# Block with four mixers on one Trainium2 core: head norms by strips, and delta-rule operands in exchanged halves

## The reference

```python
def l2norm(x, eps=1e-6):
    return x * rsqrt(sum(x * x, axis=-1) + eps)

def gated_deltanet(qkv, a_logit, b_logit, z, ...):
    q, k, v = split(silu(causal_depthwise_conv(qkv, conv_w)))
    q = l2norm(heads(q)) * HEAD_DIM ** -0.5
    k = l2norm(heads(k))
    g = -exp(a_log) * softplus(a_logit + dt_bias)
    o = chunked_gated_delta_rule(q, k, v, g, sigmoid(b_logit))
    return rmsnorm(o, norm_w) * silu(heads(z))

def spatial_gating(u, v, z, ...):
    v = layernorm(heads(gelu(v)), ln_gain, ln_bias, 1e-5)
    mixed = einsum('gts,bnsgc->bntgc', tril(w_s), v) + b_s
    return gelu(u) * mixed * silu(z)

def rwkv7_time_mix(rw, z, mu, ...):
    rw = rw + mu * (shift_prev(rw) - rw)
    r, k, v, wd, ad = split(rw)
    decay = exp(-exp(-softplus(-(w0 + tanh(wd) @ w_up)) - 0.5))
    a = sigmoid(a0 + ad @ a_up)
    kk = l2norm(heads(k * k_k))
    k = k * (1 + (a - 1) * k_a)
    o = rwkv7_scan(r, decay, k, v, kk, a)
    o = layernorm(o, gn_gain, gn_bias, 64e-5) + sum(r * k * r_k, -1) * v
    return o * silu(z)
```

## Time and profile before

| what | value |
|---|---|
| median of 3 runs | 2642.43 us (2641.89 to 2644.74) |
| the profiled execution, its own time | 2643.93 us |
| span of its trace | 2642.6 us |
| mean granted clock of TensorE | 0.958 |
| TensorE (PE) busy | 2408.1 us, 91% |
| weight loads (PEld) busy | 1046.9 us, 40%, beside PE |
| VectorE (DVE) busy | 930.5 us, 35% |
| ScalarE (ACT) busy | 497.8 us, 19% |
| DMA | 556.51 MB, mean 211 GB/s |

### The profile page before, as it was taken

How to read it: one execution, slowest core, us unless ns; L and a number is a source line. 1 busy time by engine, 2 the same in 40 slices (tenths; PEclk the granted TensorE clock), 3 DMA queues, 4 the chain that set the end, 5 groups by cost and what they waited for, 6 DMA issues and landing times.

```text
span 2642.6 us, 27853 instructions
## 1 busy us (share of the span) xinstructions
PE 2408.1 (91%) x11714; PEld 1046.9 (40%) x11714; DVE 930.5 (35%) x1538; ACT 497.8 (19%) x823; POOL 0.2 (0%) x4
## 2 busy tenths in 40 slices
PE   6899989699999999986999999989998699998698
PEld 1344345233333333432333333334443246754443
DVE  4548652411111115644012111131017755417652
ACT  2246100211011011022101101120014322114500
POOL 0000000000000000000000000000000000000000
PEclk9899999899999999998999999989999899998799
DMA  7134411599999974415899999912222111023042
GB/s 280 72 143 151 159 64 56 211 421 421 421 422 421 421 316 191 173 66 208 350 421 421 421 421 422 406 38 79 72 76 74 48 61 50 24 64 121 1 159 80
DMA packets 96858, 556.51 MB, mean 211 GB/s; under 512 B 13561, under 2 KB 14073, under 8 KB 40219
## 3 DMA queue, kind: packets, MB, share of 16 engines
q1 hardware_dynamic: 90432, 538.77, 51.7%
q10 hardware_dynamic: 6300, 15.95, 1.6%
HBM read 544.19 MB, written 10.49 MB: 210 GB/s over the span
## 4 chain that ended last, share of the span: by engine, by line
PE 80%; DVE 13%; ACT 4%; issue 2%; DMA 0%; ACTq 0%; DVEq 0%; SPq 0%
PE bank L205 78%; PE bank L208 2%; DVE residual L1371 1%; DVE rms L1709 1%; DVE scores L2465 1%; DVE proj L431 1%; DVE topk L1267 0%; DVE squares L1337 0%; DVE max L1266 0%; ACT squares L1331 0%; ACT wring L1299 0%; ACT L1668 0%; ACT scores_t L2510 0%; DVE cf_y L1563 0%; DVE proj L1709 0%
## 5 line engine op out<-in xcount | busy, mean ns | idle before, releaser
L205 PE MATMUL bank<-normed,wring 128*128 128x512 f32 x1712 | 779.3, 607 | 11.1 <-DVE proj_small L2676 3.8
L205 PEld LDWEIGHTS bank<-normed,wring 128*128 128x128 f32 x1712 | 322.6, 193 | 408.1 <-issue 392.6
L205 PE MATMUL bank<-experts,wring 128*64 128x512 f32 x2048 | 445.8, 593 | 1.8 <-ACT wring L1313 1.8
L1337 DVE TENSOR_TENSOR squares<-squares,bank 128x512 f32<-128x512 f32 x32 | 22.0, 688 | 676.1 <-ACT squares L1331 676.1
L205 PEld LDWEIGHTS bank<-experts,wring 128*64 128x64 f32 x2048 | 145.5, 137 | 287.0 <-issue 284.8
L205 PE MATMUL bank<-experts,hs_t 128*64 128x512 f32 x1024 | 223.3, 594 | 1.5 <-ACT hs_t L1352 1.5
L205 PE MATMUL bank<-give_t,y 128*128 128x512 f32 x256 | 128.6, 621 | 10.2 <-DVE residual L1371 5.9
L205 PEld LDWEIGHTS bank<-experts,hs_t 128*64 128x64 f32 x1024 | 72.1, 137 | 141.3 <-issue 139.4
L1371 DVE SCALAR_TENSOR_TENSOR residual<-bank,mods,residual 128x512 f32<-128x512 f32 x128 | 96.1, 751 | 69.9 <-PE bank L205 64.2
L205 PE MATMUL bank<-h_tm,pick 128*128 128x512 f32 x256 | 117.6, 614 | 2.4 <-DVE pick L1279 2.4
L205 PE MATMUL bank<-proj,wring 128*128 128x512 f32 x224 | 99.4, 597 | 1.6 <-DVE proj L2563 1.6
(11 more groups left out here) (469 smaller groups left out, 2090.4 us busy)
## 6 DMA issues: line engine op xcount, KB each, us to landing
experts<-in_exp_w SPq DMA_DIRECT2D x384, 1024.0 KB, 15.1
wring<-in_w_in SPq DMA_DIRECT2D x82, 512.0 KB, 3.5
residual<-in_w_mod SPq DMA_DIRECT2D x24, 1024.0 KB, 6.6
cf_wmod<-in_w_mod SPq DMA_DIRECT2D x16, 1024.0 KB, 5.7
wring<-in_cf_w SPq DMA_DIRECT2D x24, 512.0 KB, 3.5
wmod<-in_w_mod SPq DMA_DIRECT2D x8, 1024.0 KB, 10.0
merge_gates<-squares ACTq DMA_DIRECT2D x32, 256.0 KB, 2.5
proj<-merge_gates SPq DMA_DIRECT2D x8, 1024.0 KB, 6.4
```

The lines of the kernel that those rows point to most:

```text
L205: return self.nc.tensor.matmul(out, lhsT, rhs, start=start, stop=stop, skip_group_check=True)
L1337: k.vec(v.tensor_tensor(m.hs[:, e, :], m.hs[:, e, :], k.bank[3 - 2 * e][:, :], ALU.mult), f"{m.name}.hs{i}.{e}")
```

## The change

**Head norms.** For the sums of squares, four products of 128x32 (stationary, from a new constant tile `heads`) by 128x128 a chunk put the chunk's sums in four strips of 32 partitions of one 128x128 tile: row 32g + 8i + 4h is token group g, chunk i, head h (`head_strips_tensor`). Up to four chunks add into the same tile. One mean, one root and one reciprocal of 128x128 follow (`head_roots`), then VectorE spreads the roots over 512 columns (L1743 of the changed kernel), and one product of 128x512 a chunk spreads them over the head's rows (`head_spread_tensor`). VectorE scales from PSUM with the gain in the same instruction (`head_scaled_vector`). The squares are made on ScalarE (`head_square_scalar`). The spatial mixer's bias is added on ScalarE. The sums for centring stay as they were, but the four Gelus are in another order (the two that are waited for come first), and one more DMA (`heads`, 128x644) is issued ahead of them. In gdn's preparation six more filler steps are drawn in its six convolution rounds; the spatial mixer draws one step fewer.

**Delta rule.** `m` and `u` of the levels are written to the other half of the partitions (`OTHERS`) by products whose input and output halves differ, and so are `x` of the chunks, the transposed `bv` of gdn, and the first level's transposed copies, for which there is a second set of 64x512 products. `products_tensor` takes several products and interleaves them: `m` of pair p+1 and `t` of pair p go call by call. The order is now m0, (m1, t0), u0, (m2, t1), u1, (m3, t2), u2, t3, u3.

**Memory.** `rw_up` and `rw_scratch` have no buffers of their own any more and lie in `mixer_out`.

The diff, cut:

```diff
+def head_constants():
+
+
+    p, j = np.arange(P)[:, None], np.arange(32)[None, :]
+    sums = [(j // 8 == i) * (j % 8 // 4 == p // 64) for i in range(4)]
+    rows = [p % 32 == 8 * i + 4 * (np.arange(P)[None, :] // 64) for i in range(4)]
+    return np.concatenate(sums + rows + [p // 32 == np.arange(4)[None, :]], 1).astype(np.float32)
...
-        self.up = d.sb("rw_up", [P, 256])
-        self.z3 = d.sb("rw_scratch", [P, T])
+        self.z3, self.up = self.ys[:, 4, :], self.ys[:, 5, 0:256]
...
+def head_strips_tensor(k, m, name, i, after, src, b, last):
+    t = k.nc.tensor
+    t.wait_ge(*k.at(after))
+    for g in range(4):
+        ins = k.mm(k.bank[b][32 * g:32 * g + 32, 0:P], m.heads[:, 32 * i:32 * i + 32], src[:, g * P:(g + 1) * P], i == 0, last)
+    if last:
+        ins.then_inc(*k.up("tensor", f"{name}.strips"))
...
+    k.vec(v.reciprocal(rt, rt))
+    k.vec(v.tensor_tensor(fm3(rs, 4), rt.unsqueeze(1).broadcast_to([P, 4, P]),
+                          m.heads[:, 640:644].unsqueeze(2).broadcast_to([P, 4, P]), ALU.mult), f"{name}.roots")
...
+def head_spread_tensor(k, m, name, i, rs, b):
+    k.nc.tensor.wait_ge(*k.at(f"{name}.roots"))
+    k.mm(k.bank[b][:, :], m.heads[:, (i + 1) * P:(i + 2) * P], rs).then_inc(*k.up("tensor", f"{name}.spread{i}"))
...
+def head_scaled_vector(k, name, i, x, gain, b):
+    v = k.nc.vector
+    v.wait_ge(*k.at(f"{name}.spread{i}"))
+    k.vec(v.scalar_tensor_tensor(out=x, in0=x, scalar=gain, in1=k.bank[b][:, :], op0=ALU.mult, op1=ALU.mult), f"{name}.scaled{i}")
...
-def gdn_prepare_tensor(k, m):
+def squares_of(m):
+    return m.kh[:, 0, :], m.kh[:, 1, :], m.bv[:, 0, :], m.bv[:, 1, :]
+
+
+def gdn_prepare_tensor(k, m, filler):
     t, bank, PJ, SL = k.nc.tensor, k.bank, m.pj, m.sl
     B, BB, E = (PJ[:, 8 + i, :] for i in range(3))
-    yield from steps_of(6)
-    for c in range(4):
-        yield from head_sums_tensor(k, f"gp.sum{c}", f"gp.sq{c}", B, 0)
-        yield
+    for c in range(6):
+        if 1 <= c <= 4:
+            head_strips_tensor(k, m, "gp", c - 1, f"gp.sq{c - 1}", squares_of(m)[c - 1], 0, c == 4)
+        next(filler, None)
+        yield
+    yield
+    yield
+    head_spread_tensor(k, m, "gp", 0, m.ys[:, 1, :], 1)
+    head_spread_tensor(k, m, "gp", 1, m.ys[:, 1, :], 2)
+    yield
+    t.wait_ge(*k.at("gp.scaled1"))
+    head_spread_tensor(k, m, "gp", 2, m.ys[:, 1, :], 1)
+    head_spread_tensor(k, m, "gp", 3, m.ys[:, 1, :], 2)
...
+        if c < 4:
+            head_square_scalar(k, f"gp.sq{c}", f"gp.silu{c}", squares_of(m)[c], PJ[:, c, :])
+        next(filler, None)
...
+    head_mean_vector(k, "gp", 0, 1.0, 1e-6, m.rt[:, 0, :])
+    yield
+    head_root_vector(k, m, "gp", m.rt[:, 0, :], m.ys[:, 1, :])
+    yield
+    for c in range(2):
+        head_scaled_vector(k, "gp", c, PJ[:, c, :], HD ** -0.5, 1 + c)
+    yield
+    for c in range(2, 4):
+        head_scaled_vector(k, "gp", c, PJ[:, c, :], 1.0, c - 1)
     v.wait_ge(*k.at("gp.silu5"))
-    for c in range(4):
-        k.vec(v.tensor_tensor(B, PJ[:, c, :], PJ[:, c, :], ALU.mult), f"gp.sq{c}")
-        yield
-        v.wait_ge(*k.at(f"gp.sum{c}"))
-        yield from root_vector(k, f"gp.norm{c}", bank[0][:, :], 1.0, 1e-6, E)
-        if c < 2:
-            k.vec(v.scalar_tensor_tensor(out=PJ[:, c, :], in0=PJ[:, c, :], scalar=HD ** -0.5, in1=E, op0=ALU.mult, op1=ALU.mult))
-        else:
-            k.vec(v.tensor_tensor(PJ[:, c, :], PJ[:, c, :], E, ALU.mult))
...
-        k.vec(v.tensor_scalar(kk, key, k.vector_of("rw_k_k_2", p), None, ALU.mult))
-        k.vec(v.tensor_tensor(e, kk, kk, ALU.mult), f"rp{p}.sq")
-        yield
-        v.wait_ge(*k.at(f"rp{p}.sum"))
-        yield from root_vector(k, f"rp{p}", bank[6][:, :], 1.0, 1e-6, e)
-        k.vec(v.tensor_tensor(kk, kk, e, ALU.mult))
+        v.wait_ge(*k.at(f"rp.spread{p}"))
+        k.vec(v.scalar_tensor_tensor(out=kk, in0=key, scalar=k.vector_of("rw_k_k_2", p), in1=bank[6][:, :], op0=ALU.mult, op1=ALU.mult))
...
-def products_tensor(k, name, b, left, right):
+def products_tensor(k, *products):
+
+    last = {}
     for n in range(NCH):
         c = slice(n * CH, (n + 1) * CH)
-        for r in HALVES:
-            ins = k.mm(k.bank[b][r, c], left[r, c], right(r, c))
-    ins.then_inc(*k.up("tensor", name))
+        for name, b, left, right, change in products:
+            for r, o in zip(HALVES, OTHERS if change else HALVES):
+                last[name] = k.mm(k.bank[b][o, c], left[r, c], right[r, c])
+            if n == NCH - 1:
+                last[name].then_inc(*k.up("tensor", name))
...
     def second(lv, p):
         t.wait_ge(*k.at(f"lv{lv}.mm{p}"))
+        return f"lv{lv}.t{p}", p, d.mm[:, p, :], d.tt[:, p, :], False
+
+    def third(lv, p):
         if lv < LEVELS - 1:
             take_tensor(k, 4 + p)
-            products_tensor(k, f"lv{lv}.u{p}", 4 + p, d.tt[:, p, :], lambda r, c: d.mm[r, p, c])
-        products_tensor(k, f"lv{lv}.t{p}", p, d.mm[:, p, :], lambda r, c: d.tt[r, p, c])
+            products_tensor(k, (f"lv{lv}.u{p}", 4 + p, d.tt[:, p, :], d.mm[:, p, :], True))
 
     for lv in range(1, LEVELS):
-        for p in range(4):
-            first(lv, p)
-            if p:
-                second(lv, p - 1)
-        second(lv, 3)
+        products_tensor(k, first(lv, 0))
+        for p in range(1, 4):
+            products_tensor(k, first(lv, p), second(lv, p - 1))
+            third(lv, p - 1)
+        products_tensor(k, second(lv, 3))
+        third(lv, 3)
...
-            for r in HALVES:
+            for r, x in zip(HALVES, OTHERS):
                 if p >= 2:
-                    k.mm(bank[0][r, o], m.aak[r, p - 2, c], m.vv[r, p - 2, c], True, False)
-                ins = k.mm(bank[0][r, o], m.til[r, p, c], d.g[r, p, :], p < 2, True)
+                    k.mm(bank[0][x, o], m.aak[r, p - 2, c], m.vv[r, p - 2, c], True, False)
+                ins = k.mm(bank[0][x, o], m.til[r, p, c], d.g[r, p, :], p < 2, True)
```

214 lines of the change are left out of this document (139 added, 75 removed).

## The result

| | before | changed |
|---|---|---|
| median | 2642.71 us (2641.89 to 2644.74, 4 runs) | 2620.03 us (2616.00 to 2623.67, 4 runs) |
| ratio | | 0.9913, interval 0.9898 to 0.9929 |
| profiled execution (span) | 2643.93 (2642.6) | 2619.75 (2618.4) |
| TensorE busy | 2408.1 | 2394.1 |
| VectorE busy | 930.5 | 880.8 |

The account below looks back on a forecast made before the run. TensorE, 80% of the chain of waits, was taken to bound the kernel. Savings of 5.0 + 19.9 + 9.1 less 7.4 made 26.6 us; 2643.9 - 26.6 = 2617.3, less 1.5 for the median: 2616 us, range 2604 to 2635.

Parts of the forecast that it names:

- The likeliest case: Whole kernel: the forecast of 2616 us holds, own range 2608 to 2624; chance 0.60.
- Spatial mixer: Stage with the first head norm: one short reciprocal replaces two and one filler step goes; 5.0 us less, from 43.8.
- Preparation: Stage before the levels: shorter norm chain, TensorE's hole moved to the bonus; 19.9 us less, 199.5 to 179.6.
- the last two scalings on VectorE: 52.6: Preparation: rounds, roots, reciprocals and spreads end with VectorE's scalings 52.6 us into the stage, before the softplus.
- the third rival: Early chain of the preparation: ScalarE reaches the gdn root late, half of the 19.9 us goes, total 2626; chance 0.13.
- Levels: Levels of the inverse: woven m and t overlap, each level 13.56 to 11.7 us; 9.1 us less, 71.3 to 62.2.
- Chunks: Chunk stage: x and u in crossed quarters, same calls and filler steps; no change from 92.0 us.
- Keys: Keys and finishes: four strip sets and four filler steps more, some waits covered; 7.4 us more, 51.0 to 58.4.
- The rule against the weave: Levels: the skill's floor of about 25 ns between starts makes a woven pair 1.6 us and the total 2626.
- The first rival: Levels: the weave does not overlap, a pair costs 1.86 us, levels take 79.2, total 2633; chance 0.20.
- The second: Levels, preparation, chunks: crossed quarters do not run two at a time, 45 us over 48 products, total 2678; chance 0.05.

Follow-up runs that it names:

- e12: e6 plus the ring, with one of the two filler steps before the first gdn kh product moved before the preparation's first spread; 2592.5 us, ratio 0.9810.
- e8: Changed kernel without the six filler steps drawn in the convolution rounds of gdn's preparation; 2621.5 us, ratio 0.9924.
- e2: Kernel before with only the exchanged halves of the delta rule, head norms as before; 2629.0 us, ratio 0.9959.
- e7: Changed kernel, weave kept but m written to the half it reads from, so woven m and t share the straight quarters (another inverse); 2628.7 us, ratio 0.9950.
- e4: Changed kernel with gdn's softplus, its factor and the cumulative sum moved from the preparation into the projections; 2607.1 us, ratio 0.9872.
- e5: Changed kernel with eight more filler steps drawn before the first bonus product, in TensorE's 19.5 us hole; 2613.6 us, ratio 0.9891.
- e6: e4 plus four filler steps in the preparation, two before the first bonus and two before the first gdn kh product; 2595.9 us, ratio 0.9826.
- the ring: Changed kernel with m of pair 0 of the next level woven with t of pair 3 instead of standing alone; 2618.7 us, ratio 0.9909.
- e11: e6 plus the ring, with one filler step more, before the preparation's first spread; 2598.6 us, ratio 0.9828.

## Why the prediction came out as it did

The forecast was 2616 us in a range of 2604 to 2635, and faster by over 0.2% with a chance of 0.90; it is 2620.0. The likeliest case was the right one, and the sum was 2.4 us too large (26.6 against 24.2 of the profiled executions). That it missed by so little is in part luck: the preparation alone missed by 5.4, and 1.4 in the chunks, 1.3 outside the five stages, 0.7 in the keys and 0.3 in the spatial mixer, less 0.7 in the levels, made up 3.0 of it.

- **Spatial mixer**: 5.0 predicted, 5.3 measured. The first transposition starts 23.9 us into the stage, 24.9 was the figure. What follows it was not "as before": the clock is 0.5 from 2005.7 on, and the last set of `sg_w` products takes 1.71 us instead of 1.09.
- **Preparation**: 19.9 predicted, 14.5 measured. This is the term that was mis-sized. The shape was right: the hole of TensorE was moved and grown, 19.5 us at the bonus where 20 was said; from the start of the softplus to its end 15.1 us, as said (2066.30 to 2081.36); rwkv's half behind it 5.2. The failed step is the one in front, "the last two scalings on VectorE: 52.6": VectorE's last scaling ended at 57.4. Rounds of three steps and a strip set took 5.70 us, not 5.4, and here the sum itself was wrong: three steps of 1.75 and a strip set of 0.4 are 5.65. The first three steps took 7.20 instead of 5.42, since the half clock from 2005.7 on lasted 6.8 us and reached into them; so the second rwkv strip set ended at 34.4, not 31. Then the clock fell again behind a wait of 2.6 us which I had not got in the sum, and spread, rw_up and step took 1.49, 2.08 and 2.24. e12 shows that avoiding this is worth 1.9 us, e8 shows the rounds to be TensorE's. The later marks are late by 5 to 7 us (first gdn kh 94.3 for 89, second bonus 152.6 for 146, end 185.0 for 179.6). I had charged the half clock only behind the large hole; the third rival (the early chain slips) named the place but not the cause, as the roots came in the order forecast.
- **Levels**: 9.1 predicted, 8.4 measured. The woven pair at 1.08 was measured at 1.09. The level shown took 11.73 us from take to take (2211.72 to 2223.45), as forecast, but by errors that cancel: the wait for m0's copy cost 0.66, not 0.9, and crossed next to straight saved 0.17, which I did not know; a level without a gap is 11.33 (the first one). The next two took 11.87 and 11.80. The 0.4 in between is a gap for which the profile names no wait: u of pair 2 and t of pair 3 take 2.27 us to the next take (2219.95 to 2222.22) where they need 1.84, with 0.21 of it marked "issue".
- **Chunks**: 0 predicted, 1.4 measured, by that same 0.17 a chunk. "TensorE is busy for 91.4 of 92.0" was read as if busy time could not shrink. e2, which has only the exchanged halves, shows the 1.4 as well.
- **Keys**: 7.4 more predicted, 6.7 measured.

**The rule against the weave.** The woven pair has 64 records in 1.16 us, the last of which lasts 0.22: 0.94 us for 63 starts is 15 ns from start to start, held for whole products in each level. The Trainium skill (TensorE: Matmul & The Clock Gate, section "Wait — 56ns, not 53.3ns?") gives about 25 ns as a floor of the start-to-start time of products, however few columns they have; by it a pair takes 1.6 us, an estimate from that figure. The trace disagrees where all four quarters take part. In two quarters that take turns (e7) the rate is 2.08 less 0.22 over 63, 30 ns.

The first rival is refuted by the row of 1.09 us. The second, crossed quarters taking turns, is refuted by the same row and by the product that stands alone in crossed quarters (2215.00, 1.15 us as before). The first rival's price was too high as well: e7, where a pair does cost 2.01 us, has levels of 74.6 us, 11.7 above the changed kernel's, where 79.2 and 17.0 were said; fifteen pairs at 0.93 are 14, and the copies' waits, already in the forecast, were put on top again. The lower end of the range has a slip too: a preparation at 26 and levels at 12 give 2607, not 2604.

## What to carry to other kernels

When a shorter chain is put behind another one on the same engine, find what is late next and what it costs: here 19.5 us stood behind a softplus on four partitions that depended on nothing near it, and moving it to where its engine was idle was worth about half as much as the whole change. Filler is a budget: a step is worth its time in a hole only as long as the place it is taken from still has cover for its own waits, and a rule that rounds the steps up belongs in the count. Small products that leave part of the array idle are worth pairing with products in the other quarters, call by call.

## What the hardware showed that I had not expected

- Two streams of 64x64 products, one straight and one crossed, run at 15 ns a record, the time of one stream (1.09 us for both, 1.84 apart, 2.01 woven in the same quarters). Even unwoven, the seam between a crossed and a straight product is 0.17 us shorter.
- In levels with such pairs TensorE sometimes stands still for 0.2 to 0.9 us with no wait recorded, in the pairs and in single products: the same levels code took between 62.9 and 65.1 us (the changed kernel, e2, e4, e5, e6 and e8), with 2.0 us of such gaps in e6's levels, and the ring between 61.6 and 64.3. The cause is open.
- A wait of only 2.6 us, with TensorE busy before and after it, was followed by half clock in all nine kernels that had it, and a wait of 0.9 in the same place was not (e11, e12). Shorter waits were followed by it in some executions only: 1.34 us at the start of the chunks in five of fourteen, 2.07 us in the keys in five of twelve. What decides between them is open. In a long hole the lower clock is free, in work behind a short one it is not: what matters is where it falls.
